# Reading the moving operand of 9,216 matmuls in alternating blocks of 16 tokens, and moving the rooms around it

## The reference, cut to what matters

```python
x = x + s5_mixer(rms_norm(x), w_in, ..., w_glu)         # state space mixer
x = x + conv_ffn(rms_norm(x), w_up, conv_w, conv_b, w_down)
x = x + sigmoid(rms_norm(x) @ ple_w_gate) * (p @ ple_w_proj)
k, v = shared_kv(x, kv_w)                               # then differential attention
x = x + diff_attention(rms_norm(x), k, v, ..., w_q, w_o)
x = x + conv_ffn(...); x = x + gate * (p @ ple_w_proj)
x = x + even_mixer(rms_norm(x), ev_w_in, ev_w_out)      # top-k attention and pooling
x = x + (silu(h @ w1) * (h @ w3)) @ w2
x = x + odd_mixer(rms_norm(x), od_w_qkv, od_w_out)      # stick-breaking attention
x = x + (silu(h @ w1) * (h @ w3)) @ w2
```

## The kernel before, in words

| | w_hi0 | w_hi1 | w_hi2 | w_lo0 | w_lo1 | w_lo2 | opnd0 | opnd1 |
|---|---|---|---|---|---|---|---|---|
| before | 128 | 192 | 64 | 192 | 128 | 192 | 128 | 192 |
| after | 128 | 128 | 128 | 128 | 128 | 128 | 0 | 0 |

## Time and profile before

### The profile page before, as it was taken

The page is one execution under the profiler, slowest core; times in us unless marked ns, Lnnn a source line. Parts: engine busy times, 40 slices in busy tenths (PEclk is TensorE's granted clock), DMA queues, the critical chain, the costliest instruction groups (busy, mean ns, idle before and its releaser), DMA issues.

```text
span 1309.2 us, 27666 instructions
## 1 busy us (share of the span) xinstructions
PE 1278.9 (98%) x10976; PEld 1228.8 (94%) x10976; DVE 641.3 (49%) x1163; ACT 681.7 (52%) x944; POOL 1003.9 (77%) x793
## 2 busy tenths in 40 slices
PE   6999999999999999999999999999999999999999
PEld 5889999999989889999999878999999999999998
DVE  8995575555555748555555575211113454411112
ACT  7725544444676756434446565544346666644442
POOL 1226998889677659988887794988987766989985
PEclk9999999999999999999999999999999999999999
DMA  6304675555534334555554532555554433555530
GB/s 272 130 34 163 183 260 182 176 187 192 189 135 166 125 130 170 193 179 177 189 193 142 203 134 82 199 181 190 192 185 153 165 116 130 193 193 190 185 138 33
DMA packets 33879, 217.07 MB, mean 166 GB/s; under 512 B 3683, under 2 KB 7428, under 8 KB 8196
## 3 DMA queue, kind: packets, MB, share of 16 engines
q1 hardware_dynamic: 30096, 211.14, 45.5%
q10 hardware_dynamic: 3700, 4.75, 1.5%
HBM read 213.26 MB, written 2.62 MB: 165 GB/s over the span
## 4 chain that ended last, share of the span: by engine, by line
PE 83%; DVE 8%; ACT 5%; issue 2%; POOL 1%; DMA 0%; DVEq 0%; SPq 0%; ACTq 0%; POOLq 0%
PE up L1576 18%; PE up L1578 17%; PE up L1577 17%; PE acc L1576 7%; PE acc L1578 6%; PE acc L1577 6%; PE up L1711 2%; DVE opnd L980 2%; PE side L1803 2%; ACT w_hi L511 1%; PE acc L1769 1%; ACT opnd L649 1%; PE side L1584 1%; DVE mix L985 1%; PE up L1842 1%
## 5 line engine op out<-in xcount | busy, mean ns | idle before, releaser
L421 POOL TENSOR_TENSOR w_lo<-ring,w_hi 128x512 fp32r<-128x512 f32 x748 | 953.4, 1309 | 222.3 <-ACT w_hi L511 219.2
L1576 PE MATMUL up<-opnd,w_hi 128*128 128x256 f32 x2064 | 588.2, 285 | 4.1 <-DVE opnd L980 1.6
L1577 PE MATMUL up<-opnd,w_lo 128*128 128x256 f32 x2064 | 578.5, 280 | 0.0
L1578 PE MATMUL up<-opnd,w_hi 128*128 128x256 f32 x2064 | 578.1, 280 | 0.0
L511 ACT ACTIVATE w_hi<-ring 128x2048 fp32r<-128x2048 f32 x188 | 359.4, 1913 | 250.1 <-PE up L1578 191.2
L1576 PEld LDWEIGHTS up<-opnd,w_hi 128*128 128x128 f32 x2064 | 388.5, 188 | 16.6 <-issue 13.8
L1577 PEld LDWEIGHTS up<-opnd,w_lo 128*128 128x128 f32 x2064 | 390.2, 189 | 1.3 <-issue 1.0
L1578 PEld LDWEIGHTS up<-opnd,w_hi 128*128 128x128 f32 x2064 | 388.9, 188 | 0.0
L1576 PE MATMUL acc<-opnd,w_hi 128*128 128x256 f32 x784 | 221.7, 283 | 1.4 <-DVE x L1226 1.2
L1578 PE MATMUL acc<-opnd,w_hi 128*128 128x256 f32 x784 | 220.6, 281 | 0.0
L1577 PE MATMUL acc<-opnd,w_lo 128*128 128x256 f32 x784 | 219.7, 280 | 0.0
(11 more groups left out here) (296 smaller groups left out, 1424.4 us busy)
## 6 DMA issues: line engine op xcount, KB each, us to landing
ring<-in_stream SPq DMA_DIRECT2D x197, 1024.0 KB, 4.8
bias_rows<-mix ACTq DMA_DIRECT2D x1, 1536.0 KB
mix<-in_s_b SPq DMA_DIRECT2D x1, 1024.0 KB, 6.3
x<-in_x SPq DMA_DIRECT2D x1, 1024.0 KB, 8.3
mix<-in_s_c SPq DMA_DIRECT2D x1, 1024.0 KB, 12.3
mix<-bias_rows ACTq DMA_DIRECT2D x1, 1024.0 KB, 5.7
out_x<-x SPq DMA_DIRECT2D x8, 128.0 KB, 1.7
mix<-in_p ACTq DMA_DIRECT2D x2, 256.0 KB, 3.5
```

Source lines behind the costliest of these rows:

```text
L421: ins = nc.gpsimd.tensor_tensor(w_l[:, cols], ring[:, r, cols], w_h[:, cols].bitcast(f32), ALU.subtract)
L1576: MM(o, l_hi, r_hi, start=start, stop=False, skip_group_check=True)
L1577: MM(o, l_lo, r_hi, start=False, stop=False, skip_group_check=True)
L1578: return MM(o, l_hi, r_lo, start=False, stop=stop, skip_group_check=True)
```

## The change

The rooms lose their pads and stand in plain order; a pad of 128 bytes ahead of `mix` (the large work area) brings `mix` to 128 and the two operands behind it to 0 modulo 256. In `three`, the moving operand and the result are seen through `blocked`: its 256 columns are read as columns 0 to 15, 128 to 143, 16 to 31, 144 to 159 and so on, and the results go to PSUM in the same order, so each lands where it did. The weights are loaded as before. Nothing else is changed: no instruction, wait or semaphore comes or goes.

```diff
-HOMES = [(0, 0, 0), (1, 1, 0), (1, 0, 16), (0, 1, 0), (1, 2, 0), (0, 2, 32)]
-OPND_PADS = (16, 16)
+HOMES = [(part, n) for part in range(2) for n in range(3)]
+MIX_PAD = 32
+BLOCK = 16
...
-        for part, n, pad in HOMES:
-            if pad:
-                sb(f"pad_{part}{n}", [P, pad])
+        for part, n in HOMES:
...
+        sb("pad_mix", [P, MIX_PAD])
...
-        sb("pad_opnd0", [P, OPND_PADS[0]])
...
-        if OPND_PADS[1]:
-            sb("pad_opnd1", [P, OPND_PADS[1]])
...
+            def blocked(v):
+
+                return v.rearrange("p (t b c) -> p b t c", t=2, c=BLOCK)
+
             def three(o, l_hi, l_lo, r_hi, r_lo, start, stop):
 
+                o, r_hi, r_lo = blocked(o), blocked(r_hi), blocked(r_lo)
```

## The result

The changed kernel takes 1347.06 us, the median of runs between 1346.39 and 1347.84, against 1311.04 us before (1310.92 to 1311.57): a ratio of 1.0274, 95% interval 1.0256 to 1.0292. It is 36 us slower. Its profiled execution has a span of 1344.6 us. First the page: busy time of each engine, which answers to the earlier trace rows.

What follows compares the result with a forecast made beforehand. TensorE, never waiting, was taken as the bound at about 117.8 ns per matmul. Gains of 63.8 + 8.7 - 1.5 = 71.0 us off 1310.93 gave 1240 us; the case's range was 1229 to 1255, and 1229 to 1348 was held at 0.82.

Steps and rivals of the forecast that it cites:

- What bounds the kernel: Whole kernel: TensorE, busy 98% of the span and waiting for no one, limited by about 117.8 ns per matmul.
- The excess is a matter of places that repeat every 256 bytes: Matmuls of `three`: about 11 ns over 106.7 arise where moving operand and next weights are read at matching SBUF places.
- The weight load advances with the blocked read: SBUF reads in `three`: both streams advance 256 bytes modulo per 53 ns, staying half a period apart, with no pass left.
- The matmul's length with no pass left: Matmuls of `three`: 108.5 ns instead of about 117.8, a gain of 9.3 ns each.
- The price of a pass, 6.67 ns: Matmuls of `three`: moving read passing the load's place costs up to 16 columns; once gives 113.3 ns, twice 120.0.
- How much of the gain reaches the end: Of 85.7 us gross over 9,216 matmuls, 71.0 us shorten the whole kernel.
- all of 143 slots and half of 39: Glu, ple and feed-forward slots give all their gain, 63.8 us; 39 attention and similar slots give half, 8.7 us.
- POOL's limit in glu: About 8 glu slots, where POOL takes 5.43 us and sets the pace: 1.5 us lost, 3 at worst.
- rival 3: Switches between halves in SBUF read or PSUM write cost 13.3 ns per matmul, making 121.8: 1348 us, chance 0.12.
- Its test, a uniform length over 5.6 us whatever the rooms: Slots of `three`: the sign by which costly switches would show in the profile after.
- rival 2: SBUF reads in `three`: streams advance together on the same place and block each other, 128.5 ns, 1410 us; chance 0.12.

Runs made afterwards that it cites:

- e9: Changed kernel, same rooms, with halves, blocks and columns within blocks read and written last to first: 1275.86 us, ratio 0.9734, 113.3 ns per matmul.
- p2: Separate TensorE-only program holding weight load and moving read each at one place modulo 256: 243.3 ns per matmul at distance 0, 216.7 at 64 and beyond.
- p1: Separate TensorE-only stretches of 96 matmuls, plain or blocked columns at eight distances: forward blocks of 16 from two halves 120.0 ns at all eight.
- p3: Separate TensorE-only stretches of 48 matmuls, moving columns in 15 orders at eight distances: plain forward read 113.3 ns at distance 64, 123 at 48.
- p4: Separate TensorE-only stretches, blocks last to first from alternating halves, distances 16 bytes apart: with columns backward too, up to 123.4 ns around 16, 113.3 from 64 to 208.
- p5: Separate TensorE-only stretches, weight columns 260 or 252 bytes apart, 512 moving columns forward or backward: peaks of 253 ns for 260 backward and 252 forward, others at most 244.
- e2: Changed kernel with its rooms but columns read and written plainly, without blocks: 1318.08 us, ratio 1.0059, 118.7 ns per matmul.
- e1: Kernel before the change with the blocks of 16 alone, its old rooms kept: 1328.92 us, ratio 1.0140, 120.0 ns in the feed-forward stages.
- e3: Changed kernel with blocks, pad ahead of the work area doubled so weights and operands share a place modulo 256: 1327.33 us, ratio 1.0128, 120.0 ns.
- e6: Changed kernel with only the PSUM results written in blocks, moving operand read plainly (results land in another token order): 1317.58 us, ratio 1.0053.
- e10: Changed kernel, same rooms, halves and blocks last to first but columns within a block forward: 1302.38 us, ratio 0.9933.
- e7: Changed kernel with halves and blocks last to first, columns within them forward, operands moved to 192 (distance 192): 1303.13 us, ratio 0.9935, 116.7 ns.
- e4: Changed kernel without blocks, operands moved to 160 (distance 224): 1305.59 us, ratio 0.9961, 116.7 ns in the feed-forward stages.
- e8: Changed kernel with halves and blocks last to first, columns forward, operands at 160 (distance 224): 1279.05 us, ratio 0.9754, 113.3 ns, some 121 in token slots.

## Why the prediction was wrong, point by point

**What bounds the kernel: right.** TensorE sets the time while it waits for nothing; every kernel of the series moved with the ns per matmul of `three`, and PE's waits stayed small (in e9 the longest is again the 6.9 us of the first DMA).

**The excess is a matter of places that repeat every 256 bytes: right in part.** p2 shows the conflict by itself (243.3 against 216.7 ns) with its period. But of the 11 ns over 106.7, 5 are no matter of places: 128 moving columns take 111.7 ns at every distance.

**The weight load advances with the blocked read: this step failed.** I named the pace of the load as assumed, and never saw that its direction was assumed as well. With forward blocks no distance is free of the excess: 120.0 ns at all eight in p1 and p3, and 120.0 to 123.3 in the kernel against the 108.5 forecast. A load that runs from the last column to the first would do this, as the two streams would then run against each other and meet wherever they start. Turning the order in the change's own rooms takes 123.3 (120.0) down to 113.3 ns (e9). That the order is what counts is shown by e9; the direction of the load itself is inferred from p3, p4 and e9, and by the peaks of p5.

**The matmul's length with no pass left: mis-sized.** I took 108.5 ns. The floor with a 128-column load is 111.7 (p2, p4), and the best that any order reached with 256 columns is 113.3. The rows I leaned on the earlier trace rows are float32 forms: the 16 in 1.75 us are transposes, and the 16 of 216 ns are the records of eight matmuls. Float32r pairs do not repeat their 108 to 109 ns. So the gain that the change was sized for, 9.3 ns, would have been 4.5 at best. The Trainium skill, page "TensorE: Matmul & The Clock Gate", section "LDWEIGHTS (loading the stationary operand)", puts the load at its columns divided by 1.2, which makes 107 ns by estimate; the trace's 111.7 is 5 ns over it.

**The price of a pass, 6.67 ns, counted one by one: not supported.** Under blocks of 16 the kernels' steady values are 113.3, 116.7, 120.0 and 123.3, in steps of half that price, and plain reads also lie between (117.8, 118.7). A plain read would cross a backward load more often than a blocked one does, and costs no more: 116.7 to 120.0 in p1, 118.7 against 123.3 in e2 and the change. The number of meetings is not the price.

**How much of the gain reaches the end: right in size.** From e2 to e9 a matmul gets 5.4 ns shorter; all of 143 slots and half of 39 give 162.5 x 48 x 5.4 = 42.1 us, and 42.2 were measured. POOL's limit in glu is there as foreseen, with 5.35 us and no room; elsewhere 5.00 us fits.

**Switches (rival 3): right in time, wrong in mechanism.** It gave 1348 from 13.3 ns over 108.5, on all 9,216 matmuls; with half of the attention slots, as the forecast had it, the same price gives 1342. Both ends of that sum were off, and they cancelled: that its time is right is luck. Its test, a uniform length over 5.6 us whatever the rooms, fits e1, e3 and after in that all are over 5.6, though they differ (5.76, 5.76 and 5.92); a uniform length is also what streams that run against each other give, so the test did not separate the two. e6 (write, nothing), p1 (blocks of 32 no cheaper than of 16) and above all e9 and e10 (the same fifteen switches, 1275.86 and 1302.38) rule it out. That blocks of 8 cost 3.3 ns more forward, and 10 more backward (126.7 against 116.7 at 128), may still be a price of switching; it is not settled.

**The streams collide (rival 2): near the truth, as a mechanism.** It needed a skew; what brings them together, by the reading above, is direction. Its price was far too high: 128.5 ns against 120.0 to 123.3.

**What stays open.** Why the changed kernel runs at 123.3 ns in the feed-forward stages and at 120.0 in the others, with the same places: the stretches of p1 gave 120.0 at all distances, and the stage settles into 123.3 in its second slot. That is no small matter: 128 x 48 x 3.3 ns are 20 of the 36 us, and e3, the same blocks on the same place, is without them (1327.33). Streams that meet at every distance explain 120.0, but not this difference between rooms. The same plain read at distance 64 kept 117.8 in p1 and 113.3 in p3, the order of e7 at 192 kept 113.3 in p3 and 116.7 in p4. A steady state seems to depend on how a stretch began; no run tells how. Nor is it known what the last 1.6 ns between 111.7 and 113.3 are, or how a plain forward read comes to 113.3 at a single distance if the load runs against it.

## What to carry to other kernels

When two readers share a memory, ask for the direction of each before arranging their distance. Here, in blocks of 16 from two halves, one order had a band of distances that worked, and its reverse had none. Where float32r matmuls with 128x128 weights run back to back, measure the gap in short stretches of TensorE alone over distance and order of the moving read; here such a stretch told the kernel's ns per matmul to 0.1 in e4, e8, e9 and e10, though it missed the 123.3 of the change, and for e7 two stretches disagreed. So measure a stretch more than once, behind different ones. And when a time lands on a rival's number, run the test that only its mechanism passes before believing it.

## What the runs showed of the hardware

- The moving operand's read and the weight load collide in SBUF where their addresses modulo 256 bytes fall into the same 64 bytes: 243.3 ns at distance 0 and 241.8 at 32 against 216.7 at 64 and beyond, with both held still (p2).
- A matmul whose load has its columns 256 bytes apart takes 216.7 ns in place of 111.7 (p2), and 231 to 233 at 252 or 260 bytes (p5); two stretches of the latter, with a mean granted clock of 0.65 and of 0.50, gave 233.5 and 233.3.
- A float32r matmul with a load of 128 columns of its own takes at least 111.7 ns, with 128 or 192 moving columns (p2, p4); with 256 it took 113.3 to 123.4 by order and distance, and 125 to 130 in backward blocks of 8 (p3, p4); 512 take 233.3 and not 213.3 in the one order measured with an ordinary tile (p2).
- Writing PSUM in alternating blocks of 16 float32 costs nothing (e6), and a plain read backward costs no more at its worst than one forward: in p3 a plain read takes 117.8 to 120.0 backward and 113.3 to 123 forward, by distance.
- A float32 matmul stands in the trace as two records (line 1743 issues eight and shows 16), and a record of 256 columns takes 216 ns at a granted clock of 1.00, the 2.4 GHz level, before and after.
